# Output projections by halves of the tokens, with three layer norms cut into halves between matmuls

## The chip, the cores and the metric

One core of one Trainium2 chip runs the whole program. The metric is device microseconds (us) of one execution. The kernel before was timed in three runs: median 2960.02 us, from 2954.51 to 2963.22.

## The reference, cut to what matters

The input is 1024 tokens of width 1024 in float32. Two layers follow, each a mixer and then a squared-ReLU MLP of width 4096, each behind an RMS norm and added to the residual:

```
def rms_norm(x, g):
    y = x * rsqrt(mean(x * x, axis=-1) + 1e-6)
    return y * g
# layer 0: z = rms_norm(h, g0) @ w_in  -> RG-LRU branch and 8-head latent attention
#          h = h + concat(lru, mla) @ w_out
#          h = h + square(relu(rms_norm(h, g1) @ w1)) @ w2
# layer 1: z = rms_norm(h, g2) @ w_in  -> native sparse attention, 16 heads
#          h = h + o @ w_out
#          h = h + square(relu(rms_norm(h, g3) @ w1)) @ w2
```

There are four norms, called norm 0 to norm 3. The change touches the two products with `w_out` and the norms 1, 2 and 3.

## The kernel before, in words

**Layout.** The residual `H` lies in SBUF channel-major: 8 chunks of 128 channels on the partitions, 1024 tokens along the free axis. A product in float32 accuracy is made of three fp32r matmuls (`mm3`, L834 to L841): high by high, high by low, low by high. So every operand has a high and a low copy. The input of a stage is `U_hi` and `U_lo`. Weights come in pieces of 128x2048 (1 MB). SyncE loads a piece into one of four slots of `W_raw`, which share their place with `W_lo`; GpSimd (POOL) makes `W_hi` by a cast (L653) and then `W_lo` by a subtraction in place (L659). Before every split the slot must be loaded, and before every load TensorE must have counted the slot's last reader in the semaphore `used` (`piece_read`: the first matmul of the next unit adds one).

**Order.** Each engine has its own program, in order, written out by hand; semaphores tie them. No planner is at work. A wait in one engine's program holds back all that stands behind it there.

**Output projection** (`out_proj`, `add_out` at L2098). 16 units, one for each of 8 output chunks and 2 token halves, of 24 matmuls of 512 columns each. Unit n computes chunk n // 2, half n % 2, into PSUM bank n % 8. The first four units run together, chunk by chunk of the input (`first_units`), since `U_lo` is only just being made (L2053 in layer 0, L2332 in layer 1). VectorE (DVE) adds each unit to `H`. After both halves of a chunk, ScalarE (ACT) squares it (1024 wide, L1406) and VectorE adds the square to `nacc` (L1779, L1782), under the matmuls of the next chunks.

**Norm** (k = 1, 2, 3). Then, one after the other: 8 small matmuls sum `nacc` over the partitions (L849), VectorE makes the mean (L1789), ScalarE the root (L1416), VectorE the reciprocal (L1791) and 8 diagonal blocks (L1794), 8 small matmuls spread these over the partitions (L853), and for each of 8 chunks VectorE scales `H` (L1805), ScalarE copies to `U_hi` (L1422), VectorE makes `U_lo` (L1799). The next stage begins with a `first_units` that follows `U_lo` chunk by chunk: four MLP units of 512 columns after norms 1 and 3, four units of 256 columns of the next input projection after norm 2. Norm 2 comes after the MLP of layer 0; there ScalarE also writes `H` to DRAM (L1414), and it waits for that before it reads the next stage's PSUM.

**MLP.** 16 steps (8 groups by 2 token halves) of up (4 units) and down (8 units `dc` of 12 matmuls). VectorE adds each down unit to `H` (L488). The last down of layer 0 is the one ahead of norm 2.

**Splits.** The pieces of a projection by `w_out` are P_OUT0 to P_OUT0 + 3 (layer 0) and P_OUT1 to P_OUT1 + 3 (layer 1). In layer 0 POOL splits the first within the attention, between its scalings of probabilities (L719, at U == 49 and 51), the second to fourth after it. In layer 1 POOL splits all four after its last scaling (L799).

## Time and profile before

| | |
|---|---|
| median of 3 runs | 2960.02 us |
| the profiled execution | 2959.71 us |
| its span, first to last instruction | 2957.9 us |
| mean granted TensorE clock | 0.966 of full speed |
| TensorE busy | 95% |
| VectorE, ScalarE, GpSimd busy | 46%, 27%, 34% |
| DMA | 163.26 MB, mean 55 GB/s |

The profiled execution lies 0.3 us below the median, so the sums of the prediction can be laid on either. In the rows below, times are us from the start of the span. A row of the timeline gives start, duration, engine, line, operation and tiles, the count of merged instructions, and in square brackets the engine's idle time before and what ended it. The granted clock is given as a share of full speed: 1.00 is 2.4 GHz, 0.50 is 1.2 GHz. fp32 matmuls such as those of L849 and L853 appear as two records each.

### The profile page before, as it was taken

To read this page: it belongs to the slowest core of one execution; us is meant where nothing else is said; L and a number is where in the kernel's file an instruction comes from. 1 tells how busy PE (TensorE), PEld (TensorE's weight loads), DVE (VectorE), ACT (ScalarE), POOL (GpSimd) and SP (SyncE) were. 2 spreads that over 40 slices of the span, in tenths; PEclk is the share of its full clock that TensorE was granted. 3 is DMA by queue.
4 is the path that set the end of the run, shared out by engine and by line. 5 is a ranking of instruction groups with operands and counts; after the bars stand their busy time and mean duration, and the time that the engine had idled before them with its cause. 6 is when DMAs were issued, how large, how long until landed. Compare 5 with 4: busy or idle time off the path is not lost. (4 is left out here: it accounts for less than half of the span.)

```text
span 2957.9 us, 39791 instructions
## 1 busy us (share of the span) xinstructions
PE 2804.9 (95%) x15944; PEld 2335.8 (79%) x15944; DVE 1352.2 (46%) x2182; ACT 796.3 (27%) x1570; POOL 1016.2 (34%) x576
## 2 busy tenths in 40 slices
PE   6999898899999999979989899999898999999999
PEld 5778566688888888869979888888776888888887
DVE  3753653344334444352047566666644244443243
ACT  2434543121101101122123266666502011011010
POOL 3233467213213333222125244444641133332131
PEclk9999999999999999989988699999998999999999
DMA  3111002101110111121323321311020101111102
GB/s 140 38 42 43 1 1 100 43 29 57 43 42 29 57 57 57 44 99 44 105 62 72 101 68 48 94 48 48 30 100 29 38 34 57 57 57 43 43 28 86
DMA packets 30714, 163.26 MB, mean 55 GB/s; under 512 B 4471, under 2 KB 4855, under 8 KB 17719
## 3 DMA queue, kind: packets, MB, share of 16 engines
q1 hardware_dynamic: 26384, 138.02, 14.6%
q10 hardware_dynamic: 4200, 23.43, 2.0%
q8 instruction: 91, 1.49, 0.2%
q14 instruction: 39, 0.32, 0.0%
HBM read 141.33 MB, written 18.14 MB: 54 GB/s over the span
## 5 line engine op out<-in xcount | busy, mean ns | idle before, releaser
L836 PE MATMUL ps<-U_hi,W_hi 128*128 128x512 f32 (+2 forms) x1552 | 615.7, 397 | 31.2 <-DVE U_lo L1799 11.5
L653 POOL CAST W_hi<-W_raw 128x2048 fp32r<-128x2048 f32 x90 | 180.8, 2008 | 1297.8 <-DMA W_raw<-in_pieces 1285.2
L840 PE MATMUL ps<-U_lo,W_hi 128*128 128x512 f32 (+2 forms) x1552 | 610.6, 393 | 0.0
L841 PE MATMUL ps<-U_hi,W_lo 128*128 128x512 f32 (+2 forms) x1552 | 610.0, 393 | 0.0
L659 POOL TENSOR_TENSOR W_lo<-W_raw,W_hi 128x2048 fp32r<-128x2048 f32 x90 | 428.3, 4759 | 7.1
L478 DVE CAST hid_hi<-sqr 128x512 fp32r<-128x512 f32 x128 | 228.8, 1787 | 402.7 <-ACT sqr L459 402.4
L836 PE MATMUL ps<-hid_hi,W_hi 128*128 128x512 f32 x1024 | 398.3, 389 | 0.0
L840 PE MATMUL ps<-hid_lo,W_hi 128*128 128x512 f32 x1024 | 398.3, 389 | 0.0
L841 PE MATMUL ps<-hid_hi,W_lo 128*128 128x512 f32 x1024 | 398.3, 389 | 0.0
L455 ACT ACTIVATE relu<-ps 128x512 f32<-128x512 f32 x128 | 76.5, 598 | 1136.5 <-PE ps L841 1136.5
L836 PEld LDWEIGHTS ps<-U_hi,W_hi 128*128 128x128 f32 (+2 forms) x1552 | 293.2, 189 | 104.0 <-issue 35.4
L488 DVE TENSOR_TENSOR H<-H,ps 128x512 f32<-128x512 f32 x256 | 175.8, 687 | 429.1 <-PE ps L841 428.3
L841 PEld LDWEIGHTS ps<-U_hi,W_lo 128*128 128x128 f32 (+2 forms) x1552 | 292.9, 189 | 65.2
L840 PEld LDWEIGHTS ps<-U_lo,W_hi 128*128 128x128 f32 (+2 forms) x1552 | 293.4, 189 | 64.1 <-issue 1.0
L799 POOL TENSOR_SCALAR PX<-PX,rinv,GATE 128x640 f32<-128x640 f32 (+7 forms) x256 | 198.6, 787 | 255.6 <-DVE rinv L2296 255.6
L841 PEld LDWEIGHTS ps<-hid_hi,W_lo 128*128 128x128 f32 x1024 | 192.2, 188 | 40.1
L836 PEld LDWEIGHTS ps<-hid_hi,W_hi 128*128 128x128 f32 x1024 | 192.2, 188 | 39.9
L840 PEld LDWEIGHTS ps<-hid_lo,W_hi 128*128 128x128 f32 x1024 | 192.2, 188 | 39.8
L1716 ACT ACTIVATE PX<-PX,nmx 128x640 f32<-128x640 f32 (+7 forms) x256 | 185.6, 731 | 2.4 <-DVE nmx L2290 1.9
L1330 PE MATMUL ps<-cs,PX 128*128 128x128 f32 x1056 | 165.7, 281 | 1.7 <-ACT PT L1725 0.4
L2304 DVE COPY PT<-ps 128x512 f32<-128x512 f32 (+1 forms) x192 | 94.6, 520 | 155.4 <-PE ps L1330 155.4
L1351 PE MATMUL ps<-PT,KV 128*64 128x128 f32 x2112 | 143.6, 278 | 4.7 <-DVE PT L2304 2.3
(290 smaller groups left out, 3934.7 us busy)
## 6 DMA issues: line engine op xcount, KB each, us to landing
W_raw<-in_pieces SPq DMA_DIRECT2D x90, 1024.0 KB, 4.8
RSB<-es_d SPq DMA_DIRECT2D x16, 512.0 KB, 6.5
QHH<-qh_d SPq DMA_DIRECT2D x32, 256.0 KB, 4.8
RWB<-ew_d SPq DMA_DIRECT2D x16, 320.0 KB, 7.7
H<-in_xT ACTq DMA_DIRECT2D x1, 4096.0 KB, 22.7
H<-in_xT ACTq DMA_DIRECT2D x2, 2048.0 KB, 7.7
h_d<-H ACTq DMA_DIRECT2D x1, 4096.0 KB, 17.0
W1C<-in_w1c SPq DMA_DIRECT2D x4, 1024.0 KB, 5.7
```

The source lines that it names most:

```text
L478: V_.tensor_copy(hid_hi[s][:, m, :], sqr[:, m % 2, :]).then_inc(hh, 1)
L488: V_.tensor_tensor(H[:, dc, cols], H[:, dc, cols], ps[:, 4 + dc % 4, :], ALU.add).then_inc(dn_free, 1)
L653: nc.gpsimd.tensor_copy(W_hi[:, k, :], W_raw[:, k, :]).then_inc(split_hi, 1)
L659: nc.gpsimd.tensor_tensor(W_lo[:, k, :], W_raw[:, k, :], W_hi[:, k, :].bitcast(F32), ALU.subtract).then_inc(ready, 1)
L799: nc.gpsimd.tensor_scalar(p, p, rinv[:, c:c + 1], GATE[:, i, hd * 3 + 1 + br:hd * 3 + 2 + br], ALU.mult, ALU.mult).then_inc(x_nm, 1)
L836: m = mm(o, a_hi, b_hi, start=first, stop=False)
L840: mm(o, a_hi, b_lo, start=False, stop=False)
L841: return mm(o, a_lo, b_hi, start=False, stop=last)
L1330: m = nc.tensor.transpose(ps[:, 4 + n % 2, kb % 4 * P:kb % 4 * P + P], PX[U % 7][:, kb * P:(kb + 1) * P], ident)
L1351: m = mm(ps[DK * e:DK * (e + 1), 6 + i // 4, i % 4 * P:i % 4 * P + P], KV[:, k0 + kb, 1 if br == SEL else 3, hd // HPG, :], PT[(2 * s + e) ...
L1716: A(p, p, ACT.Exp, bias=nmx[:, U % 16:U % 16 + 1], scale=-1.0, accum_out=sums[:, U % 32:U % 32 + 1]).then_inc(x_exp, 1)
L2304: V_.tensor_copy(PT[U % 4][:, k0 * P:k1 * P], ps[:, 4 + n % 2, 0:(k1 - k0) * P]).then_inc(x_cpv, 1)
```

## The change

What it does:
- The output projection takes the token halves in turn: units 0 to 7 are the 8 chunks of half 0, units 8 to 15 those of half 1. Banks 0 to 3 and, in turn, 4 and 5 are used; 6 and 7 are left to the norm. Only the units 0 and 1 run in `first_units`. Each piece is read until half 1, so `used` counts at the first matmuls of units 10, 12 and 14 and at the end.
- Norms 1, 2 and 3 are done in two halves of 512 tokens. VectorE: all 8 adds of half 0, then the seven accumulations of its squares, then the steps of `norm_steps`, with the adds of half 1 in between. TensorE sums the squares of half 0 after unit 8 and spreads after unit 10; for half 1 it sums within the next `first_units` after its chunk 1 and spreads after chunk 3, and waits for all of `U_lo` behind it. For norm 2 the places are the last down's units 1 and 3, and chunks 2 and 5 of the next projection, whose units use 7 banks instead of 8; three more units follow the second half.
- Layer 0: the second piece's cast stands in the attention (U == 55), its subtraction right behind it. Layer 1: the first two pieces are split within the last pair of heads; the third and fourth wait for all of `U_lo`.

The diff, cut to its core:

```diff
+        NA, ND, NU, NQ = ([at("%s%d" % (n, k), o + d, [P] + shape) for k, o in enumerate((G0, A0 + 8192))]
+                          for n, d, shape in (("nah", 0, [HALF]), ("ndh", 512, [4, P]), ("nuh", 1024, [2, HALF]),
+                                              ("nqh", 2048, [2, HALF])))
...
+        def index(k, half):
+            return 2 * k - 1 + half
+        def out_bank(n):
+            return n % 8 if n % 8 < 4 else 4 + n % 2
+        def bank_user(n):
+            return max(m for m in range(-1, n) if m < 0 or out_bank(m) == out_bank(n))
+        Z1_BANKS = (0, 1, 2, 4, 5, 6, 7)
...
+                    if isinstance(n, int) and n == MLP_UNITS - 1 and layer == 0 and dc == 1:
+                        sum_squares(2, 0)
+                    if isinstance(n, int) and n == MLP_UNITS - 1 and layer == 0 and dc == 3:
+                        spread(2, 0)
...
-            first_units(2 * layer + 1, [up_bank(m) for m in range(4)], up_ready)
+            first_units([up_bank(m) for m in range(4)], up_ready, n_lo, KC * index(k, 0),
+                        {1: lambda: sum_squares(k, 1), 3: lambda: spread(k, 1)})
+            pe.wait_ge(n_lo, KC * (index(k, 1) + 1))
...
+                if U == 6 * NT + 7:
+                    split_high(0, P_OUT0 + 1)
+            split_low(0, P_OUT0 + 1)
+            for p in (P_OUT0, P_OUT0 + 1):
+                n_loaded[p % 4] += 16
             pool.wait_ge(a_qk, M_ALL)
             pool.wait_ge(x_lo, KC)
-            split_one(P_OUT0 + 1)
             pool.wait_ge(a_t, len(M_SEQ))
             pool.wait_ge(a_pv, M_STEP)
             split_one(P_OUT0 + 2)
...
+                if U == 7 * N_U + 1:
+                    pool.wait_ge(x_qk, 7 * N_U)
+                    split_high(0, P_OUT1)
+                if U == 7 * N_U + 5:
+                    split_low(0, P_OUT1)
+                if U == 7 * N_U + 11:
+                    split_high(0, P_OUT1 + 1)
+                if U == 7 * N_U + 15:
+                    split_low(0, P_OUT1 + 1)
+            for p in (P_OUT1, P_OUT1 + 1):
+                n_loaded[p % 4] += 16
             pool.wait_ge(x_qk, N_ALL)
-            split_one(P_OUT1)
-            split_one(P_OUT1 + 1)
+            pool.wait_ge(x_lo, XL0 + KC)
             pool.wait_ge(x_t, n_chunks(N_ALL))
             split_one(P_OUT1 + 2)
             split_one(P_OUT1 + 3)
...
+            def sum_squares(k, half):
+                q = index(k, half)
+                pe.wait_ge(n_acc, 7 * (q + 1))
+                if k == 2 and half:
+                    pe.wait_ge(n_uf, KC * q)
+                for t in range(4):
+                    m = mm(ps[:, 3 if k == 2 else 6, t:t + 1], NA[k == 2][:, t * P:(t + 1) * P], ones[:, 0:1], start=True, stop=True)
+                m.then_inc(n_ssq, 1)
+            def spread(k, half):
+                q = index(k, half)
+                pe.wait_ge(n_dg, NT + 4 * q)
+                if half:
+                    pe.wait_ge(n_uf, KC * q)
+                for t in range(4):
+                    m = mm(ps[:, 3 if k == 2 else 7, t * P:(t + 1) * P], ones[:], ND[k == 2][:, t, :], start=True, stop=True)
+                m.then_inc(n_bc, 1)
+            def first_units(units, then, low, low0, between={}):
                 for kc in range(KC):
-                    pe.wait_ge(low, low0 + KC * k + kc + 1)
+                    pe.wait_ge(low, low0 + kc + 1)
                     for unit in units:
                         o, a_hi, a_lo, b_hi, b_lo = unit(kc)
                         m = mm3(o, a_hi, a_lo, b_hi, b_lo, kc == 0, kc == KC - 1)
                         if kc == KC - 1:
                             m.then_inc(then, 1)
+                    if kc in between:
+                        between[kc]()
...
+                first_units([lambda kc: unit_(0, kc), lambda kc: unit_(1, kc)], o_ready, x_lo, low0)
+                for n in range(2, 16):
+                    if n < 8 and n % 2 == 0:
+                        pe.wait_ge(ready, p0 + n // 2 + 1)
+                    if bank_user(n) >= 0:
+                        pe.wait_ge(o_added, 16 * k + bank_user(n) + 1)
+                    for kc in range(KC):
+                        m = mm3(*unit_(n, kc), kc == 0, kc == KC - 1)
+                    m.then_inc(o_ready, 1)
+                    if n in (9, 11, 13):
                         piece_read()
+                    if n == 8:
+                        sum_squares(2 * k + 1, 0)
+                    if n == 10:
+                        spread(2 * k + 1, 0)
                 piece_read_now(o_ready, 16 * (k + 1))
...
+            pe.wait_ge(dn_free, 4 + 8 * MLP_UNITS - 3)
+            first_units([z1_unit(t) for t in range(4)], z_ready, n_lo, KC * index(2, 0),
+                        {2: lambda: sum_squares(2, 1), 5: lambda: spread(2, 1)})
+            pe.wait_ge(dn_free, 4 + 8 * MLP_UNITS)
+            first_units([z1_unit(t) for t in range(4, 7)], z_ready, n_lo, KC * index(2, 1))
...
+                    for t in range(7 if p == P_IN1 else 0, NT):
+                        pe.wait_ge(z_evac, n - 6 + Z0)
...
+            def squares(k, half):
+                q = index(k, half)
+                for c in range(KC):
+                    if k == 2:
+                        act.wait_ge(dn_free, 4 + 8 * (MLP_UNITS - 2 + half) + c + 1)
+                        act.wait_ge(dn_ready, 1 + 8 * (MLP_UNITS - 1))
+                    else:
+                        act.wait_ge(o_added, 16 * (k // 2) + 8 * half + c + 1)
+                    if c >= 2:
+                        act.wait_ge(n_acc, 7 * q + c - 1)
+                    elif half:
+                        act.wait_ge(n_acc, 7 * q)
+                    A(NQ[k == 2][:, c % 2, :], H[:, c, half * HALF:(half + 1) * HALF], ACT.Square).then_inc(n_sq, 1)
+            def normed(k, half):
+                q, cols = index(k, half), slice(half * HALF, (half + 1) * HALF)
+                act.wait_ge(n_ms, q + 1)
+                A(msq[:, 8 + 4 * half:12 + 4 * half], msq[:, 4 * half:4 * half + 4], ACT.Sqrt).then_inc(n_sd, 1)
+                for c in range(KC):
+                    act.wait_ge(n_uf, KC * q + c + 1)
+                    A(U_hi[:, c, cols], NU[k == 2][:, c % 2, :], ACT.Copy).then_inc(n_hi, 1)
             def norm(k):
+                squares(k, 0)
+                normed(k, 0)
+                squares(k, 1)
                 if k == 2:
-
                     act.wait_ge(dn_free, 4 + 8 * MLP_UNITS)
                     act.dma_start(h_d[:, :, :], H[:]).then_inc(h_spill, 16)
+                normed(k, 1)
...
+            def diagonals(k, half):
+                q = index(k, half)
+                dve.wait_ge(n_sd, q + 1)
+                V_.reciprocal(rsd[:, 4 * half:4 * half + 4], msq[:, 8 + 4 * half:12 + 4 * half]).then_inc(n_rs, 1)
+                dve.wait_ge(n_rs, q + 1)
+                for t in range(4):
+                    V_.tensor_scalar(ND[k == 2][:, t, :], ident, rsd[:, 4 * half + t:4 * half + t + 1], None, ALU.mult
+                                     ).then_inc(n_dg, 1)
+            def low(k, half, c):
+                q, cols = index(k, half), slice(half * HALF, (half + 1) * HALF)
+                dve.wait_ge(n_hi, KC * q + c + 1)
+                V_.tensor_tensor(U_lo[:, c, cols], NU[k == 2][:, c % 2, :], U_hi[:, c, cols].bitcast(F32), ALU.subtract
+                                 ).then_inc(n_lo, 1)
+            def scaled(k, half, g0, c):
+                q, cols = index(k, half), slice(half * HALF, (half + 1) * HALF)
+                if c == 0:
+                    dve.wait_ge(n_bc, q + 1)
+                if c >= 2:
+                    dve.wait_ge(n_lo, KC * q + c - 1)
+                V_.scalar_tensor_tensor(NU[k == 2][:, c % 2, :], H[:, c, cols], pr[:, g0 + c:g0 + c + 1],
+                                        ps[:, 3 if k == 2 else 7, :], ALU.mult, ALU.mult).then_inc(n_uf, 1)
+                if c >= 1:
+                    low(k, half, c - 1)
+            def norm_steps(k, g0, add):
+                a, sq, q = NA[k == 2][:], NQ[k == 2], index(k, 0)
+                for c in range(1, KC):
+                    add_squares(a, sq, q, c)
+                add(0)
+                if k == 2:
+                    add(1)
+                mean(k, 0)
+                if k != 2:
+                    add(1)
+                add(2)
+                diagonals(k, 0)
+                add(3)
+                for c in range(KC):
+                    scaled(k, 0, g0, c)
+                    if c in (1, 3, 5):
+                        add(4 + c // 2)
+                low(k, 0, KC - 1)
+                for c in range(1, KC):
+                    if c == 6:
+                        add(7)
+                    add_squares(a, sq, q + 1, c)
+                mean(k, 1)
+                diagonals(k, 1)
+                for c in range(KC):
+                    scaled(k, 1, g0, c)
+                low(k, 1, KC - 1)
...
+                V_.tensor_tensor(H[:, c, cols], H[:, c, cols], ps[:, out_bank(n), :], ALU.add).then_inc(o_added, 1)
+            for n in range(8):
+                add_out(0, n)
+            norm_steps(1, G_MLP0, lambda c: add_out(0, 8 + c))
```

## Rows read from the trace of the kernel before

**Rows 1.** Timeline of PE within norm 1.

```profile
576.16 3.58 PE L849 MATMUL ps<-ones,nacc 128*128 128x1 f32 x16 [4.32 <-DVE nacc L1782]
...
585.23 3.59 PE L853 MATMUL ps<-ndiag,ones 128*128 128x128 f32 x16 [5.50 <-DVE ndiag L1794]
```

**Rows 2.** Timeline of DVE and ACT, before and after norm 1.

```profile
571.87 0.69 DVE L2098 TENSOR_TENSOR H<-H,ps 128x512 f32<-128x512 f32 x1 [4.75 <-PE ps L841]
...
615.52 0.60 ACT L455 ACTIVATE relu<-ps 128x512 f32<-128x512 f32 x1 [8.37 <-PE ps L841]
```

**Rows 3.** Timeline of DVE and ACT, before and after norm 3.

```profile
2228.20 0.69 DVE L2098 TENSOR_TENSOR H<-H,ps 128x512 f32<-128x512 f32 x1 [4.75 <-PE ps L841]
...
2271.49 0.60 ACT L455 ACTIVATE relu<-ps 128x512 f32<-128x512 f32 x1 [7.95 <-PE ps L841]
```

**Rows 4.** Timeline of DVE and ACT, before and after norm 2.

```profile
1298.78 0.69 DVE L488 TENSOR_TENSOR H<-H,ps 128x512 f32<-128x512 f32 x1 [0.89 <-PE ps L841]
...
1341.44 0.38 ACT L1622 ACTIVATE SQR<-ps 128x256 f32<-128x256 f32 x1 [1.58 <-PE ps L841]
...
1344.33 0.38 ACT L1622 ACTIVATE SQR<-ps 128x256 f32<-128x256 f32 x1 [2.22 <-PE ps L841]
```

**Rows 5.** Windows of PE: us, busy (x), granted clock, DMA share, GB/s.

```profile
592.60:599.00 6.40, 6.37 (x16) 0.52 0.00 0
2148.70:2151.70 3.00, 2.92 (x7) 0.50 0.00 0
```

**Rows 6.** Timeline of ACT and DVE: a last square, its sum; a 512-wide square.

```profile
573.79 1.06 ACT L1406 ACTIVATE nsq<-H 128x1024 f32<-128x1024 f32 x1 [9.50 <-DVE nacc L1782]
574.88 1.23 DVE L1782 TENSOR_TENSOR nacc<-nacc,nsq 128x1024 f32<-128x1024 f32 x1 [1.18 <-ACT nsq L1406]
...
L459 ACT ACTIVATE sqr<-relu x128: 631/632/637, 616.2 to 2911.9; 128x512 f32<-128x512 f32 x128
```

**Rows 7.** Timeline of POOL and DVE within the MLP of layer 0.

```profile
716.16 2.10 POOL L653 CAST W_hi<-W_raw 128x2048 fp32r<-128x2048 f32 x1
718.34 4.93 POOL L659 TENSOR_TENSOR W_lo<-W_raw,W_hi 128x2048 fp32r<-128x2048 f32 x1
...
716.54 2.27 DVE L480 TENSOR_TENSOR hid_lo<-sqr,hid_hi 128x512 fp32r<-128x512 f32 x1
718.73 4.83 DVE L478 CAST hid_hi<-sqr 128x512 fp32r<-128x512 f32 x1
```

**Rows 8.** Timeline of DVE: the 8 diagonals in norm 0 and in norm 1.

```profile
57.54 1.66 DVE L1794 TENSOR_SCALAR ndiag<-cs,rsd 128x128 f32<-128x128 f32 x8
...
580.45 4.73 DVE L1794 TENSOR_SCALAR ndiag<-cs,rsd 128x128 f32<-128x128 f32 x8
```

**Rows 9.** Timeline of SP and POOL: a load and its cast.

```profile
506.97 0.35 SPq L528 DMA_DIRECT2D W_raw<-in_pieces  x1
...
512.00 1.90 POOL L653 CAST W_hi<-W_raw 128x2048 fp32r<-128x2048 f32 x1 [0.71 <-DMA W_raw<-in_pieces]
```

**Rows 10.** The page: the scalings (L799) and the write of `H`.

```profile
L799 POOL TENSOR_SCALAR PX<-PX,rinv,GATE 128x640 f32<-128x640 f32 (+7 forms) x256 | 198.6, 787 | 255.6 <-DVE rinv L2296 255.6
...
h_d<-H ACTq DMA_DIRECT2D x1, 4096.0 KB, 17.0
```

**Rows 11.** DVE and PE where the projection of layer 1 begins.

```profile
2128.34 29.89 DVE L2332 TENSOR_TENSOR U_lo<-ZQ,U_hi 128x1024 fp32r<-128x1024 f32 x8 [0.88 <-ACT U_hi L1750]
...
2132.17 0.77 PE L836 MATMUL ps<-U_hi,W_hi 128*128 128x512 f32 x1 [5.44 <-DVE U_lo L2332]
```

**Rows 12.** POOL, DVE and PE where that of layer 0 begins.

```profile
468.82 3.11 POOL L719 TENSOR_SCALAR MX<-MX,rinv 128x512 f32<-128x512 f32 x2 [0.55 <-DVE rinv L2034]
...
477.89 1.18 POOL L719 TENSOR_SCALAR MX<-MX,rinv 128x128 f32<-128x128 f32 x2 [0.34 <-DVE rinv L2034]
...
481.73 2.36 DVE L2053 TENSOR_TENSOR U_lo<-lr,U_hi 128x1024 fp32r<-128x1024 f32 x2 [0.62 <-PE ps L1050]
...
483.10 0.77 PE L836 MATMUL ps<-U_hi,W_hi 128*128 128x512 f32 x1 [1.41 <-DVE U_lo L2053]
```

More of the change, by code:

```diff
@@ L500, in mlp_dve @@
             add(MLP_UNITS - 2, 0)
-            add(MLP_UNITS - 1, 1, True)
+            if layer:
+                add(MLP_UNITS - 1, 1)
+            else:
+                norm_steps(2, G_MIX1, lambda dc: add_one(MLP_UNITS - 1, 1, dc))
         SP_COUNT = 27
@@ L886, in _ @@
                     m.then_inc(b_ready, 1)
-            norm(0)
+            norm0()
             pe.wait_ge(ready, P_IN0 + 1)
@@ L900, in z0_unit @@
                 return operands
-            first_units(0, [z0_unit(n) for n in range(4)], z_ready)
+            first_units([z0_unit(n) for n in range(4)], z_ready, n_lo, 0)
             piece_read()
@@ L1104, in _ @@
             out_proj(P_OUT0, 0, 0)
-            norm(1)
-            mlp_pe(pe, first_units, mm3, piece_read, pieces_read_now, P_MLP0, 0)
-            norm(2)
+            mlp_pe(pe, first_units, mm3, piece_read, pieces_read_now, sum_squares, spread, P_MLP0, 0)
             pe.wait_ge(ready, P_IN1 + 1)
@@ L1377, in _ @@
             out_proj(P_OUT1, 1, XL0)
-            norm(3)
-            mlp_pe(pe, first_units, mm3, piece_read, pieces_read_now, P_MLP1, 1)
+            mlp_pe(pe, first_units, mm3, piece_read, pieces_read_now, sum_squares, spread, P_MLP1, 1)
         @block.scalar
@@ L1431, in _ @@
             act.dma_start(ew_d[:, :], esb[:, ES_N:ES_N + EW_N]).then_inc(b_out, 16)
-            norm(0)
+            norm0()
             act.wait_ge(sp_dve, 1)
@@ L1809, in norm, with mean @@
                 low(KC - 1)
+            def mean(k, half):
+                dve.wait_ge(n_ssq, index(k, half) + 1)
+                V_.tensor_scalar(msq[:, 4 * half:4 * half + 4], ps[:, 3 if k == 2 else 6, 0:4], 1.0 / D, EPS, ALU.mult, ALU.add
+                                 ).then_inc(n_ms, 1)
+            def diagonals(k, half):
[3 more added lines that the diff above has]
+                dve.wait_ge(n_rs, q + 1)
+                if half:
+                    dve.wait_ge(n_bc, q)
+                for t in range(4):
+                    V_.tensor_scalar(ND[k == 2][:, t, :], ident, rsd[:, 4 * half + t:4 * half + t + 1], None, ALU.mult
+                                     ).then_inc(n_dg, 1)
@@ L1818, in _ @@
             dve.wait_ge(const_in, 32)
-            norm(0, G_MIX0)
+            norm0(G_MIX0)
             n_sp = [0]
@@ L2333, in _ @@
                                  U_hi[:, c, :].rearrange("p (t n) -> p t n", t=NT).bitcast(F32), ALU.subtract).then_inc(x_lo, 1)
-            add_out(1)
-            norm(3, G_MLP1)
-            mlp_dve(dve, add_squares, 1)
+            for n in range(8):
+                add_out(1, n)
+            norm_steps(3, G_MLP1, lambda c: add_out(1, 8 + c))
+            mlp_dve(dve, norm_steps, 1)
 def layouts(inp):
```

181 lines of the change are left out of this document (72 added, 109 removed).

## The prediction

> **What bounds the kernel now.** I read the summary first: TensorE is busy 95% of the span, so the time is its matmuls plus the places where it stands or runs at the lower clock. Then the timeline of TensorE around a norm. In norm 1 it stands 4.32 us before 8 small matmuls of 3.58, 5.50 before 8 more [rows 1], and once more before the first `U_lo`. The reader is to see that nothing else of TensorE's lies in there: the norm is serial. What it costs is read from the units on either side. VectorE gets the last unit of the projection at 571.87; the first of the MLP's first four units is done at 615.5 [rows 2], and the other three end three matmuls apart each. A matmul takes 0.227 us (a unit of 24 takes 5.44, which is VectorE's 4.75 of waiting and 0.69 of adding [rows 2]), so the four end 2.04 later, at 617.5. That is 45.7 us for matmuls worth 4 x 5.44 = 21.8: **norm 1 costs 23.9**. The same for norm 3: 2271.5 + 2.0 - 2228.2 - 21.8 = **23.6** [rows 3]. For norm 2 the first seven units of the next projection end at 1344.33 + 2.89, and seven units are worth 7 x 2.89 = 20.2: 1347.2 - 1298.8 - 20.2 = **28.2** [rows 4]. So the change works on 75.7 us.
>
> Three things set what it pays for them. **The clock**: after TensorE has stood a few us it goes on at 1.2 GHz, for 6.4 us after norm 1's last gap, for 3.0 us in another place [rows 5]; I take 4.6, near the middle, and keep both as ends. **A chain between two engines**: a square on ScalarE (0.63 at 512 wide), 0.03, its accumulation on VectorE, 0.09 (the square of 573.79 ends 0.03 before the sum at 574.88; 0.63 is ScalarE's square of another tile of that size [rows 6]). An accumulation of 512 columns is taken like the add of 512, 0.69 [rows 2]. One step is 1.44. **POOL against VectorE**: a VectorE instruction that reads two SBUF tiles, or copies within SBUF, stands until the POOL instruction in progress ends. The one of 716.54 takes 2.27 and ends with POOL's cast, the next takes 4.83 and ends with POOL's subtraction, which had been waiting and went first [rows 7]. The 8 diagonals take 1.66 alone and 4.73 beside POOL [rows 8].
>
> **The change, part by part.**
>
> *Norms 1 and 3, half 0 (all times from the end of unit 7).* VectorE first adds unit 7 (0.7), then makes all seven accumulations; the rule in ScalarE's waits makes squares and accumulations alternate: 0.7 + 0.6 + 6 x 1.44 = 9.9. TensorE is through unit 8 at 5.44, then its program waits, and units 9 to 15 with it: **4.6**. The 4 sums are half of 3.58 [rows 1]: 1.8 (0.9 if they were twice as fast at 2.4 GHz). At the lower clock for 4.6 us, of which 1.8 are the sums, the big matmuls lose (4.6 - 1.8) / 2 = 1.4.
>
> *The spread after unit 10.* VectorE adds unit 10 before it makes the diagonals, so they start 0.96 after its end (add 0.7, reciprocal 0.2). If VectorE is free they take 0.8: TensorE stands 1.8. But unit 10's first matmul also releases the first piece's slot. In the kernel before this took 506.97 to 512.00 from issue to cast [rows 9], and the issue 0.5 after that matmul; so POOL casts from 5.5 to 7.4 after the start of unit 10 and subtracts until 12.1. The diagonals start at 6.4. One passes between the two, three after: 12.7, against 5.44: **7.3**, with spread 1.8 and clock 1.4.
>
> The boundary is a matter of 0.1 us: POOL's cast ends at 718.26 and its subtraction starts at 718.34 [rows 7], and a diagonal takes 0.2. Were the four diagonals to run on in one go once the cast is through, they would be done at 8.2 and the stand would be 2.8. The row shows the next VectorE instruction stopped, so I keep 7.3 and 2.8 is a rival.
>
> The Trainium skill (SBUF — State Buffer, "Who interferes with whom") says that whichever of the two is issued first holds the shared ports for its whole length: by that rule the stand is 7.3 if the subtraction is issued ahead of the second diagonal, and 2.8 if the wait for its cast's semaphore puts it behind all four.
>
> *Half 1 (from the end of unit 15).* Half 0's scalings and copies are hidden under units 11 to 15 (8 pairs of about 1.4, and three adds), but two of its `U_lo` meet the third piece's splits, and the last is done at +2.6. Accumulations start at 3.2. The fourth piece is released at 0: cast 5.4 to 7.3, subtraction to 12.0. They stop the third and the fourth accumulation (8.0, 12.7); three more steps: 17.0. TensorE has done two chunks of the MLP's first units at 5.44: **11.6**, plus sums 1.8 and clock 1.4. Without POOL it would be 3.3. Then 5.44 covers mean, root and diagonals; spread 1.8; the last four chunks (10.9) nearly cover 8 pairs: 0.5.
>
> Together 4.6 + 1.8 + 1.4 + 7.3 + 1.8 + 1.4 + 11.6 + 1.8 + 1.4 + 1.8 + 0.5 = **35.4** instead of 23.9 and 23.6: +11.5 and +11.8.
>
> *Norm 2.* Half 0's chain begins when the last-but-one down ends and takes 10.6; TensorE has done two down units by 5.4: 5.2, sums 1.8, clock 1.4, spread 1.8 (the diagonals are ready, POOL has no piece). Half 1's chain begins about 4 after the last down, and TensorE wants it 4.3 after (three chunks of 4 units). The last down releases two pieces: casts and subtractions from 5.5 to 18.7 stop four accumulations, the last ends near 21.5: 17.2, sums 1.8, clock 1.4, spread 1.8, and 1.4 until the three later units have followed `U_lo`. Sum **33.8** instead of 28.2: +5.6. Without POOL 25.0. The write of `H` (17.0 [rows 10]) is issued at the last square and ends before ScalarE has copied half 1; if it took 4 longer, it would show. Seven banks instead of eight cost nothing: ScalarE needs 0.8 of each 2.89.
>
> *Start of the projection, layer 1.* Now all eight `U_lo` lie beside POOL's four splits and take 29.9, one for each POOL instruction [rows 11]. After the change POOL waits for them: alone they take 1.18 each (2.36 for two [rows 12]), less than the 1.36 that two units take for a chunk. Before: matmuls start at 2132.17, and the last unit is with VectorE at 2228.20: 96.0 for 16 x 5.44 = 87.0. After: start 2129.6, 87.0 and 2.3 for the clock: 2218.9: **-9.3**. The reload of `H` is issued earlier too. The splits now stand in the last heads: POOL's idle time there is 255.6 over 128 steps, 2.0 a step [rows 10], a subtraction takes 4.6, so each may be 2.6 late; TensorE lags POOL by a step: I take +1.0 of 0 to 5.2.
>
> *The same in layer 0.* POOL had 0.55 idle before 468.82 [rows 12]; the cast of 1.9 makes the rest 1.35 later. The last scaling ends at 479.07 + 1.35; the subtraction runs from there, 480.4, to 485.0, and the first `U_lo` (481.73 before [rows 12]) ends at 486.1. Matmuls start at 486.2 instead of 483.10, and the longer stand costs 0.8 more of the clock: **+3.9** (1.4 if the subtraction met nothing).
>
> **Costed at nothing.** The slots are released at units 10, 12, 14 and 16 instead of 4, 8, 12 and 16, so SyncE loads the MLP's pieces later, and the third and fourth splits wait behind POOL's new wait for `U_lo`. Pieces three and four of the projection are ready long before units 4 and 6; the MLP's up pieces 10 us before its start, its down pieces over 20 us before the first down; without that lead each would cost up to its load and split, 5.0 + 6.6. The MLP's loop and, but for the splits, both attentions are untouched.
>
> **The sum**: 11.5 + 11.8 + 5.6 - 9.3 + 1.0 + 3.9 = +24.5. 2959.7 + 24.5 = **2984 us**. The profiled execution lies at the median of the runs, so this stands against both. With the slow stretch at 3.0 or 6.4 instead of 4.6 the norms change by 6 us either way: 2977 to 2993.
>
> **The rivals.**
>
> *POOL and VectorE miss each other, and the change is faster.* If the releases come a few us later (or the chains earlier), the spread's stand is 1.8 and half 1's 3.3, and norm 2's 8.5: 20.2, 20.2 and 25.0 instead of 23.9, 23.6, 28.2. With -9.3, +1.0 and +3.9 the sum is -14.9: **2945**. It decides at two points: POOL's cast would have to start over 0.9 after my 5.5 in unit 10, and the fourth piece 6 later than my 5.4. The load of [rows 9], 5.0, speaks against. For: 4.73 is the only diagonal of this kind I have.
>
> *The diagonals run on* between POOL's cast and its subtraction: stands of 2.8 instead of 7.3 in norms 1 and 3, -9, and -12 if so short a stand keeps the clock: 2972 to 2975, **2974**. One stopped instruction in [rows 7] is against it, the 0.08 us of the boundary for it. It is what the Trainium skill's rule named above would give in the second of its two orders.
>
> *Only the second halves miss the splits.* 8.3 and 8.3 and 8.8 less: **2959**, no change to be measured.
>
> A measurement of this kernel can tell about 0.3%, 9 us, from no change.
>
> **How the numbers follow.** The forecast 0.55, the fast rival 0.22, the diagonals 0.13, the second halves 0.10. The likeliest is the first, so 2984; its own range is 2975 to 2995. Cases of both signs have weight, so the range goes down to the fast one: 2944 to 2995. Slower: 0.55 and most of 0.13, 0.66. Same: 0.12. Faster: 0.22.
>
> **What would show it.** In the timeline of TensorE, before the sums after unit 8, a stand of 4 to 5 us on an accumulation; before the spread after unit 10 one of 7, on a diagonal of over 4 us in VectorE's rows; before the second sums one of 11 to 12 with accumulations of several us. In layer 1, `U_lo` of 1.2 each. I am wrong if these stands are under 3 us, or if TensorE keeps 2.4 GHz through them.

## The result, and the profile after

The changed kernel takes **2988.61 us** (median of 4 runs, 2984.52 to 2989.76), the kernel before beside it 2957.27 (4 runs): a ratio of 1.0101, 95% interval 1.0080 to 1.0123. It is slower by 1%. Profiled execution against profiled execution it is 2988.0 - 2959.7 = +28.3 us; forecast were +24.5 and 2984.

The page's summary after the change (busy us, share of the span, instructions):

```profile
span 2986.1 us, 39974 instructions
PE 2811.9 (94%) x15944; PEld 2340.3 (78%) x15944; DVE 1377.1 (46%) x2257; ACT 804.7 (27%) x1621; POOL 1011.2 (34%) x576
```

TensorE does the same 15944 matmuls; it is busy 7 us longer, which is the lower clock, and the rest of the loss is standing. In the rows of this document those that lie between the ones shown are left out. The timeline of TensorE in the changed kernel shows where, in norm 1 (it answers to [rows 1]) and, behind the dots, norm 2:

```profile
541.19 1.87 PE L903 MATMUL ps<-ones,nah 128*128 128x1 f32 x8 [4.64 <-DVE nah L1861]
563.23 2.08 PE L913 MATMUL ps<-ndh,ones 128*128 128x128 f32 x8 [6.82 <-DVE ndh L1903]
611.04 1.87 PE L903 MATMUL ps<-ones,nah 128*128 128x1 f32 x8 [11.00 <-DVE nah L1861]
619.91 1.06 PE L913 MATMUL ps<-ndh,ones 128*128 128x128 f32 x8
632.51 0.49 PE L877 MATMUL ps<-U_hi,W_hi 128*128 128x512 f32 x1 [0.65 <-DVE U_lo L1910]
...
1303.32 1.87 PE L903 MATMUL ps<-ones,nah 128*128 128x1 f32 x8 [5.69 <-DVE nah L1861]
1345.65 1.87 PE L903 MATMUL ps<-ones,nah 128*128 128x1 f32 x8 [16.39 <-DVE nah L1861]
```

The brackets are the stands. In norm 1 they are 4.64, 6.82 and 11.00 us; in norm 2 (the last two rows) 5.69 and 16.39. L903 are the sums of a half, L913 its spread. Norm 3 repeats norm 1 within 0.1.

The timeline of VectorE and of POOL in the changed kernel, around the second of these stands and around the third (the diagonals answer to [rows 8]):

```profile
556.45 0.69 DVE L2241 TENSOR_TENSOR H<-H,ps 128x512 f32<-128x512 f32 x1 [4.75 <-PE ps L882]
557.26 5.92 DVE L1903 TENSOR_SCALAR ndh<-cs,rsd 128x128 f32<-128x128 f32 x4
...
557.26 1.09 DVE L1903 TENSOR_SCALAR ndh<-cs,rsd 128x128 f32<-128x128 f32 x1
558.47 4.51 DVE L1903 TENSOR_SCALAR ndh<-cs,rsd 128x128 f32<-128x128 f32 x1
...
556.38 1.89 POOL L681 CAST W_hi<-W_raw 128x2048 fp32r<-128x2048 f32 x1 [49.58 <-DMA W_raw<-in_pieces]
558.35 4.55 POOL L687 TENSOR_TENSOR W_lo<-W_raw,W_hi 128x2048 fp32r<-128x2048 f32 x1
...
599.31 2.43 DVE L1861 TENSOR_TENSOR nah<-nah,nqh 128x512 f32<-128x512 f32 x1 [0.76 <-ACT nqh L1481]
602.49 4.15 DVE L1861 TENSOR_TENSOR nah<-nah,nqh 128x512 f32<-128x512 f32 x1 [0.76 <-ACT nqh L1481]
607.40 0.69 DVE L1861 TENSOR_TENSOR nah<-nah,nqh 128x512 f32<-128x512 f32 x1 [0.76 <-ACT nqh L1481]
...
599.30 1.89 POOL L681 CAST W_hi<-W_raw 128x2048 fp32r<-128x2048 f32 x1 [3.95 <-DMA W_raw<-in_pieces]
601.27 4.82 POOL L687 TENSOR_TENSOR W_lo<-W_raw,W_hi 128x2048 fp32r<-128x2048 f32 x1
```

The row of the four diagonals (x4) is their sum; the two rows under it are the first and the third alone. The first takes 1.09, until POOL's cast has ended at 558.27. The second is done by 558.55. The third, which begins at 558.47, takes 4.51, until the subtraction has ended at 562.90, and the fourth takes 0.27. So two of the four were through around the boundary, and the other two did not run on. The accumulations do the same: the one of 2.43 ends 0.55 after the cast's end, the one of 4.15 ends 0.55 after the subtraction's, and one takes 0.69 when POOL is quiet. The Trainium skill (SBUF — State Buffer, "Who interferes with whom") has it that the instruction issued first holds the shared ports for its whole length. These rows agree: the subtraction began at 558.35, 0.12 before the third diagonal.

TensorE of the changed kernel in stretches (columns: the stretch, its length, busy time and count, granted clock, DMA share, GB/s; it answers to [rows 5]):

```profile
540.00:545.00 5.00, 3.81 (x13) 0.60 0.02 3
545.00:550.00 5.00, 5.00 (x17) 0.72 0.00 0
560.00:565.00 5.00, 1.77 (x9) 0.65 0.00 0
565.00:570.00 5.00, 5.00 (x17) 0.67 0.00 0
610.00:615.00 5.00, 3.96 (x13) 0.50 0.00 0
615.00:620.00 5.00, 5.00 (x21) 0.89 0.00 0
```

0.50 is 1.2 GHz. Of 545 to 550 it is 2.8 us, so after the first stand TensorE went on at the lower clock until 547.8, 6.6 us; after the second until 568.3 (5.1), after the third until 616.1 (5.1).

**Where the 28.3 us are.** The tables of this document cut the program at the same events: P, the start of the output projection of layer 0; N1, from there to the first relu of the MLP; N2, from the last relu of that MLP to the eighth unit of layer 1's first projection; CA, layer 1's compressed attention, from the small transposes ahead of its first scores to those that stand 2 us ahead of the loop over the heads; ST, that loop (the stream of heads) and the wait for the projection; N3, as N1 in layer 1; M, the two MLPs and all that lies between these. In us against the profiled execution of the kernel before:

| | P | N1 | N2 | CA | ST | N3 | M | all |
|---|---|---|---|---|---|---|---|---|
| kernel before | 483.1 | 132.4 | 94.8 | 169.0 | 438.2 | 139.3 | 1501.1 | 2957.9 |
| the change | +2.0 | +13.9 | +6.1 | +2.6 | -1.4 | +6.6 | -1.5 | +28.2 |

### The profile page after: what moved, and what is told of

The parts are those of the page before. It is cut to its first block and busy times, and to the rows that moved or that the text cites. A ratio compares the mean times of both kernels' runs of the same rounds, so it can differ in the third digit from the quotient of the medians.

```text
span 2986.1 us, 39974 instructions
## 1 busy us (share of the span) xinstructions
PE 2811.9 (94%) x15944; PEld 2340.3 (78%) x15944; DVE 1377.1 (46%) x2257; ACT 804.7 (27%) x1621; POOL 1011.2 (34%) x576
## 5 line engine op out<-in xcount | busy, mean ns | idle before, releaser
L877 PE MATMUL ps<-U_hi,W_hi 128*128 128x512 f32 (+2 forms) x1552 | 618.6, 399 | 20.9 <-PE ps L882 9.6
## 6 DMA issues: line engine op xcount, KB each, us to landing
h_d<-H ACTq DMA_DIRECT2D x1, 4096.0 KB, 13.1
```

The costliest lines, as they stand in the source:

```text
L877: m = mm(o, a_hi, b_hi, start=first, stop=False)
```

## The experiments

Twelve runs follow, of ten new kernels and of two that are run again. The medians of the kernel before in the three sessions were 2955.25, 2955.28 and 2954.62. All stage differences are against the same profile of before; the last column leaves CA out, for a reason that the last two runs give.

| | P | N1 | N2 | CA | ST | N3 | all | without CA |
|---|---|---|---|---|---|---|---|---|
| the change | +2.0 | +13.9 | +6.1 | +2.6 | -1.4 | +6.6 | +28.2 | +25.6 |
| hold | +2.4 | -2.3 | -3.4 | -5.1 | -1.4 | -8.4 | -19.1 | -14.0 |
| order | +3.6 | -2.7 | +5.0 | +1.3 | -1.4 | -11.1 | -6.8 | -8.1 |
| order_hold | +1.5 | -12.5 | -3.4 | -5.1 | -1.4 | -18.4 | -40.2 | -35.1 |
| before_split1 | +0.2 | 0.0 | -0.2 | -3.5 | -1.5 | -7.6 | -12.6 | -9.1 |
| before_split0 | +1.4 | -0.4 | -0.2 | +2.3 | 0.0 | -0.1 | +2.8 | +0.5 |
| before_hold | +0.2 | -4.2 | -4.7 | +2.7 | +0.1 | -3.0 | -8.9 | -11.6 |
| loose | +3.3 | +6.8 | +1.4 | -15.2 | -1.4 | -1.6 | -8.0 | +7.2 |
| best | +1.2 | -18.4 | -19.4 | -4.3 | -1.4 | -25.9 | -68.1 | -63.8 |
| best_early | +1.4 | -18.9 | -20.9 | +3.7 | -1.3 | -26.4 | -62.3 | -66.0 |
| best_nohold | +1.8 | -7.1 | -11.8 | +1.2 | -1.4 | -13.8 | -31.3 | -32.5 |

**hold: is it POOL?** The change, with POOL waiting (the waits alone, put together):

```diff
+    pool.wait_ge(n_dg, NT + 4 * index(k, 0))      # before the first MLP piece of norms 1 and 3
+    pool.wait_ge(n_lo, KC * (index(k, 1) + 1))    # before the third (and in norm 2 before P_IN1 + 2)
```

> The changed kernel, with POOL's splits kept away from the norms: in norms 1 and 3 the first MLP piece's cast waits for the first half's diagonals and the third and fourth pieces wait for the second half's U_lo; in norm 2 the last two released pieces wait likewise. Theory (VectorE stands behind POOL's splits, and TensorE behind VectorE): the stand before the spread falls from 6.8 to 1 to 2 us, the one before the second sums from 11.0 to 3 to 4 in norms 1 and 3, and from 16.4 to about 8.5 in norm 2. That is 2 x (5 + 7.5) + 8 = 33 us off 2988: 2955, or 2951 if the clock gives back 1 to 2 us a norm. Rival (the chain between ScalarE and VectorE is as long as this by itself, POOL only happens to be beside it): the stands keep 6 and 10 us and the time is 2985 to 2990. A second rival: the held pieces come too late for the first down or for the unit that needs them, and a stand of several us appears before a matmul that reads W_lo.

Measured: 2942.83 us, ratio to before 0.9965 (0.9951 to 0.9979). Without CA it is 39.6 less than the change, where 33 to 37 were expected; CA is 7.7 less too, which the edit doesn't touch. The timeline of TensorE with hold, in norm 1 and, last, before norm 2's second sums:

```profile
542.07 1.56 PE L918 MATMUL ps<-ones,nah 128*128 128x1 f32 x8 [4.63 <-DVE nah L1876]
559.14 1.16 PE L928 MATMUL ps<-ndh,ones 128*128 128x128 f32 x8 [1.78 <-DVE ndh L1918]
596.05 1.05 PE L918 MATMUL ps<-ones,nah 128*128 128x1 f32 x8 [2.50 <-DVE nah L1876]
...
1321.11 1.87 PE L918 MATMUL ps<-ones,nah 128*128 128x1 f32 x8 [7.53 <-DVE nah L1876]
```

6.82 became 1.78, 11.00 became 2.50, and 16.39 in norm 2 became 7.53; the first stand, which owes nothing to POOL, is 4.63 as before. No held piece came late. The rival, a chain that is as long by itself, falls.

**order: is it the place of the small steps?**

```diff
-                    if n == 8:
+                    if n == 9:
                         sum_squares(2 * k + 1, 0)
...
                 if k != 2:
+                    diagonals(k, 0)
                     add(1)
                 add(2)
-                diagonals(k, 0)
+                if k == 2:
+                    diagonals(k, 0)
```

> The changed kernel with only the places of the first half's norm moved in norms 1 and 3: the sums stand after unit 9 instead of 8, and VectorE makes the diagonals before it adds units 9 and 10, so that they lie ahead of POOL's first cast; the spread stays after unit 10. POOL is not held off. Theory (a small step of TensorE's stands only because it was put too early, and half 1's chain then starts earlier too): no stand before the first sums (was 4.6) nor before the spread (was 6.8); the second sums' stand falls from 11 to about 7, since VectorE is through with half 0 some 3 us before unit 15 ends and two splits still stop it. A norm costs about 15 instead of 37: 2 x 22 = 44 less, 2944. Rival (VectorE's and ScalarE's own chain from unit 7 to the second sums is the bound, and TensorE's early stands only moved the time about): the second stand grows to 20 to 22, and the time stays at 2985 to 2990.

Measured: 2951.94, ratio 0.9992 (0.9980 to 1.0004), no difference from the kernel before. The timeline of TensorE with order, norm 1:

```profile
543.87 0.95 PE L903 MATMUL ps<-ones,nah 128*128 128x1 f32 x8
550.27 1.06 PE L913 MATMUL ps<-ndh,ones 128*128 128x128 f32 x8
595.56 1.87 PE L903 MATMUL ps<-ones,nah 128*128 128x1 f32 x8 [11.00 <-DVE nah L1861]
```

The first two stands are gone, as expected, and with them 16.6 us of N1: 4.64 + 6.82 of standing, 1.9 of small matmuls at the lower clock (1.87 and 2.08 became 0.95 and 1.06), and 3.2 of big ones. The third was expected at 7 and is 11.00 to the hundredth as before, and 2952 was measured where 2944 was expected. So both theories were half wrong. Nothing grew to 20: the chain is not a fixed length. But VectorE gained nothing on TensorE either. These rows of order's VectorE and POOL show why:

```profile
576.09 4.93 DVE L1910 TENSOR_TENSOR U_lo<-nuh,U_hi 128x512 fp32r<-128x512 f32 x2
580.95 0.68 DVE L1858 TENSOR_TENSOR nah<-nqh 128x512 f32<-128x512 f32 x1
...
574.93 4.95 POOL L687 TENSOR_TENSOR W_lo<-W_raw,W_hi 128x2048 fp32r<-128x2048 f32 x1
583.83 1.89 POOL L681 CAST W_hi<-W_raw 128x2048 fp32r<-128x2048 f32 x1 [3.95 <-DMA W_raw<-in_pieces]
```

Half 1's accumulations begin 1.07 after the third piece's subtraction ends (579.88), as they do in the change (595.35 and 596.42). That piece is released by TensorE's own unit 14, the fourth by the end of unit 15. Whatever TensorE gains, the splits come as much earlier.

**order_hold: both.**

> Both edits together: the order of the run before it and POOL's splits held off as in the first. If both theories hold, norms 1 and 3 have no stand before the first sums and the spread, and 1 to 3 us before the second sums; norm 2 stands 5.7 and 8.5. 2988 - 2 x 28 - 8 = 2924, faster than both kernels. If only the order counts, 2944; if only POOL, 2955; if neither, 2988.

Measured: 2924.52, ratio 0.9907 (0.9876 to 0.9938), as expected. In norm 1 no stand over 0.7 but 2.50 before the second sums; N1 is 12.5 below the kernel before.

**before_split1: one part of the change alone**, on the kernel before:

```diff
+                if U == 7 * N_U + 1:
+                    pool.wait_ge(x_qk, 7 * N_U)
+                    split_high(0, P_OUT1)
...
-            split_one(P_OUT1)
-            split_one(P_OUT1 + 1)
+            pool.wait_ge(x_lo, XL0 + KC)
```

> The kernel before with one part of the change alone: in layer 1 the first two output pieces are split within the stream of heads, and the other two wait for U_lo. By the terms of the prediction: the stream 1.0 longer, the projection 2.6 earlier, and the eight U_lo no longer stopped by POOL, 9.3 in all: -8.3 against the kernel before (2957), 2949; in the trace the projection's matmuls start 1.6 earlier and its first four units' U_lo take 1.2 us each instead of 3.7. Rival (the first units follow U_lo anyway and the gain is lost at the next wait, or two splits of 4.6 us hold up the heads by their whole overhang, 5.2): 2954 to 2958.

Measured: 2947.50, ratio 0.9973 (0.9957 to 0.9989); without CA -9.1. The timeline of VectorE with before_split1, the row of the eight `U_lo`, which was 29.89 in [rows 11]:

```profile
2125.82 9.17 DVE L2342 TENSOR_TENSOR U_lo<-ZQ,U_hi 128x1024 fp32r<-128x1024 f32 x8 [0.88 <-ACT U_hi L1760]
```

1.15 each. Counted from the end of CA, the heads end 0.9 later, the projection starts 1.5 earlier, and the way from there to the first relu is 7.6 shorter. Of that 0.8 lies behind the projection, in norm 3, whose last stretch at the lower clock was shorter (the 6.4 us from its last gap had a granted clock of 0.73, in the kernel before 0.60). This part pays; the change gives it back elsewhere.

**loose: the alternation of square and accumulation.**

```diff
                     if c >= 2:
-                        act.wait_ge(n_acc, 7 * q + c - 1)
+                        act.wait_ge(n_acc, 7 * q + max(1, c - 2))
```

> The changed kernel with one wait made as loose as its two buffers allow: ScalarE's square c waits for accumulation c-2 instead of c-1 (all three norms); POOL as in the change. Theory (square and accumulation alternate only because of this wait): the steps go from 1.45 us to about 0.8, the stand before the first sums from 4.6 to under 1 in norms 1 and 3 and from 5.7 to about 1.5 in norm 2; the spread's stand stays 6.8, since it hangs on unit 10 and POOL; the second sums' stand goes from 11.0 to about 9. Together 2 x 6 + 5 = 17 less than 2988: 2971. Rival (an accumulation cannot follow its own predecessor faster, or POOL's splits set the end of the chain whatever the step is): steps of 1.4, or no stand changes but the first: 2979 to 2988.

Measured: 2950.62 (10 runs), ratio 0.9991 (0.9978 to 1.0005). Without CA it is 18.4 below the change, where 17 were expected; the other 17.8 lie in CA, whose instructions the edit does not touch (see the last two runs). The timeline of VectorE with loose, norm 1:

```profile
533.55 0.69 DVE L1858 TENSOR_TENSOR nah<-nqh 128x512 f32<-128x512 f32 x1
534.99 4.68 DVE L1861 TENSOR_TENSOR nah<-nah,nqh 128x512 f32<-128x512 f32 x6 [0.76 <-ACT nqh L1481]
```

Six accumulations in 4.68: five steps of 0.80 and the last one's 0.69, where a step was 1.45. Two buffers were there, and the wait used one. The rival, an accumulation that can't follow its own predecessor faster, falls. TensorE stood 1.38 instead of 4.64, and its clock was 1.00 in the 5 us that followed.

**best: all of it, and norm 2 rebuilt.** In norm 2 the second half's squares and accumulations stand between the first half's scalings:

```diff
+                    for c in range(KC):
+                        scaled(2, 0, g0, c)
+                        if c in (0, 2, 3, 4, 6):
+                            add({0: 3, 2: 4, 3: 5, 4: 6, 6: 7}[c])
+                        if c >= 2:
+                            add_squares(a, sq, q + 1, c - 1)
...
-            first_units(..., {2: lambda: sum_squares(2, 1), 5: lambda: spread(2, 1)})
+            first_units(..., {6: lambda: sum_squares(2, 1), 7: lambda: spread(2, 1)})
```

> All that the runs so far point to: POOL held off, the first half's sums after unit 9 with the diagonals ahead of the adds, the looser wait, the second spread after chunk 2 instead of 3; and norm 2 rebuilt: first sums after down unit 2 instead of 1, the second half's squares and accumulations set between the first half's scalings, second sums after chunk 6 and spread after chunk 7 of the next projection. Against the run with order and hold (2924.5): the second sums' stand of 2.5 goes to under 0.5 in norms 1 and 3 (2 x 3), and norm 2 from 24.9 (what it cost with POOL held off) to 12 or 13. 2924.5 - 6 - 12 = 2906. Rival (in norm 2 VectorE is the bound and the interleaving gives nothing): stands of 6 to 8 us move to the second sums and the time is 2914 to 2918.

Measured: 2898.34, ratio 0.9808 (0.9795 to 0.9822). The timeline of TensorE with best, norm 1 and the second half of norm 2:

```profile
541.42 0.94 PE L918 MATMUL ps<-ones,nah 128*128 128x1 f32 x8
547.82 1.06 PE L928 MATMUL ps<-ndh,ones 128*128 128x128 f32 x8
581.96 0.95 PE L918 MATMUL ps<-ones,nah 128*128 128x1 f32 x8
585.62 1.06 PE L928 MATMUL ps<-ndh,ones 128*128 128x128 f32 x8
...
1293.81 0.95 PE L918 MATMUL ps<-ones,nah 128*128 128x1 f32 x8
1296.38 1.16 PE L928 MATMUL ps<-ndh,ones 128*128 128x128 f32 x8
1299.85 0.36 PE L892 MATMUL ps<-W_hi,U_hi 128*128 128x256 f32 x1 [2.32 <-DVE U_lo L1928]
```

No bracket of more than 0.3 us is left in norm 1. N1 is 18.4 below the kernel before, where norm 1 cost 23.9. Against order_hold it is 28.7 less without CA; 18 were expected. Norm 2 gave 16 instead of 12, N1 and N3 6 and 7.5 instead of 3 each. The second stand of 2.50 had cost clock too (0.66 granted in the 5 us after it), which the expectation left out. In norm 2 the stands fell from 5.70 and 7.56 in order_hold to 2.32, which is 10.9; the two sums from 1.87 to 0.95 each, 1.8; the other 3.3 go with the clock, which was 0.59 and 0.55 in the 7 us from order_hold's two sums and 1.00 in the 10 us from 1299 in best.

**best_early and best_nohold.** The first moves two small steps, the second takes hold's waits out of best:

```diff
-            first_units(..., {6: lambda: sum_squares(2, 1), 7: lambda: spread(2, 1)})
+            first_units(..., {5: lambda: sum_squares(2, 1), 6: lambda: spread(2, 1)})
```

> The best kernel so far with norm 2's second sums after chunk 5 instead of 6 and its spread after chunk 6 instead of 7. In its trace the last accumulation is done 3 us before the sums, and the 2.3 us in which TensorE then stands before the second half's first U_lo lie behind the spread. Expected: that stand goes or falls under 0.5, 2 to 3 us less; from 2898 to 2896. Rival: the diagonals are not ready after chunk 6 (sums 1.0, mean, root and diagonals 1.9, chunk 1.4) and a new stand of 1 to 1.5 before the spread takes half of it.

Measured: **2889.97**, ratio 0.9781 (0.9762 to 0.9800), the lowest median of this study. The stand of 2.32 became 0.89, N2 1.5 shorter, and nothing stood before the spread. Most of the 8.4 by which the median lies under that of best is not the edit's: without CA the profiled executions differ by 2.2, as expected, and the runs of either kernel fall into two groups, 2888 to 2892 and 2897 to 2900.

> The best kernel without its hold on POOL: the same orders, loose wait and rebuilt norm 2, with the splits of the next pieces as soon as their loads land. If the orders alone keep the chain clear of POOL, 2898 to 2905. Theory: the first halves stay clear, but the last piece's cast and subtraction still start 5.4 us after unit 15 and meet the diagonals or the last accumulations: stands of 3 to 7 us in norms 1 and 3 before the second sums or the spread; in norm 2 two pieces meet the second half's scalings and accumulations, 6 to 9 us. Together 2898 + 2 x 5 + 8 = 2916.

Measured: 2928.45, ratio 0.9902 (0.9884 to 0.9920). The hold is worth 30 us even with the best order (31.3 by the stages without CA): 8.70 before the second sums in norm 1, and in norm 2 a stand before the spread. The timeline of TensorE with best_nohold:

```profile
591.45 1.87 PE L903 MATMUL ps<-ones,nah 128*128 128x1 f32 x8 [8.70 <-DVE nah L1864]
...
1314.88 2.08 PE L913 MATMUL ps<-ndh,ones 128*128 128x128 f32 x8 [6.74 <-DVE ndh L1906]
```

The expectation, 18 more than best, was too low by 13, nearly all of it in N1 and N3: they lose 11.3 and 12.1, not 5 each. In N1 that is 8.7 of standing, 0.9 of sums at the lower clock and 1.7 of what follows.

**before_hold: would the old order have gained as much?** The kernel before, with:

```diff
+    pool.wait_ge(n_lo, KC * (k + 1))    # before the fourth MLP piece, and in norm 2 before P_IN1 + 2
```

> The kernel before with POOL's splits kept away from its three norms, nothing else: the fourth MLP piece waits for all U_lo of norms 1 and 3, the third and fourth input piece for those of norm 2. Diagonals of 4.7, 4.7 and 5.0 us go to 1.7 and one U_lo of 2.25 to 1.2: -3 - 3 - 4 = -10, 2945. If this equals the changed kernel with POOL held off (2943, which also has the two moved splits, -8 and about +3), then halving the norms brought nothing by itself, in the order in which the change puts them. Rival (the stands of the old norms are TensorE's own small matmuls and the path over ScalarE; the diagonals lie beside them): 2953 to 2956.

Measured: 2951.41, ratio 0.9984 (0.9974 to 0.9993); without CA -11.6, where -10 was expected. The change with POOL held off (-14.0) has also the splits of layer 1 (-9.1) and of layer 0 (+0.5). Leaving these out, it is at -5.4, and the old norms with the same care at -11.6. (That the parts add up so is taken for granted; no run has the halved norms without the moved splits.) In the order in which the change put them, the halves bring nothing, POOL or not; with the order, the looser wait and the rebuilt norm 2 of best they bring over 40 us more (-63.8 + 8.6 against -11.6).

**before_split0: the layer-0 splits alone**, on the kernel before:

```diff
+                if U == 6 * NT + 7:
+                    split_high(0, P_OUT0 + 1)
+            split_low(0, P_OUT0 + 1)
...
-            split_one(P_OUT0 + 1)
```

> The kernel before with one part of the change alone: in layer 0 the second output piece's cast and subtraction move from behind U_lo into and to the end of the stream of units. By the prediction's terms the first U_lo is stopped by the subtraction, the projection starts 3.1 us later and the clock costs 0.8 more: +3.9 (by what the changed kernel's trace shows, 2.0 to 3). 2955 + 3 = 2958. Rival (U_lo gains back what the start loses, since the old cast and subtraction no longer stand in POOL after it; or the split's place does not matter): 2953 to 2956.

Measured: 2962.29, ratio 1.0019 (1.0008 to 1.0029). The projection starts 1.4 later and the first relu comes only 1.0 later; the rest of what the runs show is not in the stages that the edit touches (CA +2.3). The clock shows why it is only 1.0. TensorE in the 6 us from the projection's first matmul, in the kernel before:

```profile
483.10:489.10 6.00, 6.00 (x20) 0.75 0.96 375
```

The same 6 us with before_split0, and the 6.4 us behind the last gap of norm 1 (0.52 in [rows 5]):

```profile
484.45:490.45 6.00, 6.00 (x17) 0.61 0.77 295
594.90:601.30 6.40, 6.37 (x21) 0.73 0.00 0
```

The later start comes with a longer stand (3.09 instead of 1.41), and 6 x (0.75 - 0.61) = 0.8 us more are lost to the clock there. In norm 1, which the edit doesn't touch, 6.4 x (0.73 - 0.52) = 1.3 are won back; why is open.

**after_again and loose_again: what repeats.** No edit; the change and loose once more.

> The changed kernel itself, once more, to see which of its stretches repeat. The stretch of layer 1's compressed attention (from its first matmul to the first head of the stream) took 171.6 us, with a mean granted clock of 0.74, where the kernel before had 169.0 and other runs with the same instructions 153.8 to 171.7. If the clock there hangs on the program and its timing, it is 171 to 172 again and the whole 2984 to 2990; if it hangs on the moment, it can be anything from 154 to 172 and the whole varies with it.

> The kernel with the looser wait, once more. Its compressed attention took 153.8 us at a mean granted clock of 0.86, 18 less than the changed kernel's with the same instructions; that is half of the 36 by which it came out faster. If that hangs on the program: 153 to 155 again, 2948 to 2953. If on the moment: something else, up to 172 and 2969.

Measured: the change again 2987.21, ratio 1.0106 (1.0089 to 1.0123); the looser wait again 2957.49. Without CA the profiled executions lie at +27.0 (+25.6 the first time) and +7.8 (+7.2). CA does not repeat. One row each of TensorE over all of CA (columns as above): first the changed kernel.

```profile
1546.30:1717.90 171.60, 153.49 (x972) 0.74 0.36 87
```

The same kernel again:

```profile
1548.00:1712.80 164.80, 145.83 (x972) 0.78 0.37 91
```

The kernel with the looser wait:

```profile
1535.90:1689.60 153.70, 134.29 (x971) 0.86 0.39 97
```

And that one again:

```profile
1532.80:1696.50 163.70, 145.28 (x971) 0.78 0.38 91
```

The same 971 or 972 matmuls take 153.7 to 171.6 us at 0.86 to 0.74 of the clock. It does not hang on the program alone: loose's two profiled executions differ by 10.4 us, and CA by 9.9. The ten runs of loose are six of 2948 to 2952 and four of 2959 to 2961.

## Why the prediction was right

It forecast 2984, slower by 24.5 us, and gave "slower" 0.66. The mechanism that it gave is the one that the rows show; that the sum came out within 4 us is in part luck, since errors of 1 to 3 us had both signs. Point by point:

- **The stands.** Forecast in norm 1 were 4.6, 7.3, 11.6 and 0.5; measured 4.64, 6.82, 11.00 and 0.65. In norm 2 5.2 and 17.2; measured 5.69 and 16.39. They came from where it said, VectorE's alternation with ScalarE (steps of 1.44 forecast, 1.45 measured) and POOL's splits, and hold and loose took each away by its own edit. The rivals in which POOL and VectorE miss each other fell on the row of the cast: it began at 556.38, 0.9 before the diagonals, as forecast; the one in which all four diagonals run on fell on the third one's 4.51. The reading that one diagonal passes at the boundary was off by one, as two did; with that, and the path as forecast, the stand came out at 6.82 instead of 7.3. The evidence for it ahead of the run was one row.
- **The clock in norms 1 and 3 was under-sized.** Norm 1 costs 23.9 + 12.4 = 36.3 (the MLP's steady units come 15.28 later; of that 2.03 are the later start of the projection and 0.8 the clock behind it); forecast 35.4. Stands 23.1 (forecast 24.0) and small matmuls 6.9 (7.2) leave 6.3, where the three terms of 1.4 made 4.2. The slow stretches were 6.6, 5.1 and 5.1, not 4.6; that explains about 5.5. Most of the other 0.8 is how a bracket is counted: a matmul's row is 0.39 long, the next one could have started 0.23 after it began, so each of the four brackets is some 0.16 short. Norm 3 by the same account, set against before_split1: +13.5, forecast +11.8; 0.8 of it is the shorter slow stretch of before_split1.
- **Norm 2**: +6.1, forecast +5.6. The write of `H` took 13.1 and hid.
- **Layer 1's splits**: forecast -9.3 + 1.0; in the change +1.0 for the stream and 2.5 less of waiting; alone on the kernel before -9.1 in all, 0.8 more than forecast, and these 0.8 are that same slow stretch in norm 3.
- **The layer-0 start was over-sized.** Forecast +3.9. The stand before the projection is 3.09 instead of 1.41, and its start moved by 2.0; in before_split0 it moved by 1.4, and the whole was +1.0 at the first relu. (P itself lies between +1.2 and +3.6 in the kernels that have this split, with no difference of theirs ahead of it; the looser wait gave +3.3 and, the same program again, +1.2. So this term is not known to better than 1 us.) The step that failed is the start of the subtraction, put at 480.4 and measured at 479.39: it moved by 0.3 against the end of the last scaling (479.07), not by 1.35. The extra clock term of 0.8 is there: in the 6 us from the projection's first matmul the changed kernel was granted 0.61, the kernel before 0.75. So the start costs 2.9.
- **Not forecast**: +2.6 in CA, where the same program differs by more than that from one execution to the next.

Against the forecast these are +0.9 and +1.7 for norms 1 and 3, +0.5 for norm 2, -0.8 for the splits, -1.0 for the start and +2.6 in CA: +3.9, the difference between 24.5 and 28.3 but for 0.1.

## What to carry to other kernels

Cutting a serial step in two and laying each half under the other half's matmuls paid here only where the matmul engine came to the small step after its chain was done: count the chain, put the step behind it, and keep every wait as loose as the buffers allow. A third engine whose work is released by the covered matmuls moves along with them, so it meets the chain again at each new order; give it an explicit wait instead of hoping for a gap. And read a gain stage by stage: here 18 us of one run's 36 lay in a stretch that the edit did not touch.

## What the runs showed of the hardware

- With the same instructions, CA took between 153.7 and 172.6 us over the fourteen profiles, at a granted clock of 0.86 to 0.74; two executions of one program differed by 6.8 (the change) and 9.9 (loose). The whole range is 0.6% of the kernel's time, more than several of the edits.
- POOL's cast and its subtraction lie 0.08 us apart. Two of the four diagonals, 0.27 each, were through around that boundary. Of the eight `U_lo`, 1.2 each, only one was through for each POOL instruction, and they took 29.9 [rows 11].
- POOL stands behind VectorE too. The timeline of VectorE and of POOL with best_nohold has one cast of 3.23 instead of 1.89, beside VectorE instructions with two SBUF inputs that follow each other until 1301.86:

```profile
1301.18 0.68 DVE L1864 TENSOR_TENSOR nah<-nah,nqh 128x512 f32<-128x512 f32 x1
...
1300.39 3.23 POOL L681 CAST W_hi<-W_raw 128x2048 fp32r<-128x2048 f32 x1 [38.58 <-DMA W_raw<-in_pieces]
1303.70 4.59 POOL L687 TENSOR_TENSOR W_lo<-W_raw,W_hi 128x2048 fp32r<-128x2048 f32 x1
```

- The 4 small fp32 matmuls of a half's sums (8 in the rows) take 0.95 at 2.4 GHz and 1.87 at 1.2, those of the spread 1.06 and 2.08. The prediction took 1.8 for each; at the higher clock both are half of that. Stands of 1.38 (loose), 1.78 (hold) and 2.32 us (best) left the clock at 1.00, one of 2.50 (order_hold) was followed by 3.4 us at the lower one.
